# A two-layer decoder trunk on eight cores: small column block first, and the deferred norm steps spread over the next stage

## The reference, cut to what is computed

```
for i in range(2):                                   # layer 0 even mixer, layer 1 odd mixer
    x = x + 0.5 * swiglu(rmsnorm(x, g_ffn[i,0]), ...)        # 1024 -> 2*2816 -> 1024
    h = rmsnorm(x, g_mix[i])
    x = x + (even_mixer(h) if i == 0 else odd_mixer(h))      # pooling + 31-wide conv | 3-wide conv
    x = x + 0.5 * swiglu(rmsnorm(x, g_ffn[i,1]), ...)
    gate = sigmoid(rmsnorm(x, g_ple[i]) @ w_ple_gate[i])
    x = x + gate * rmsnorm(p[i] @ w_ple_proj[i], g_pp[i])
y = rmsnorm(x, g_final)
```

## Time and profile before

| what | value |
|---|---|
| time before, median of 2 runs | 3115.78 us (3113.93 to 3117.63) |
| the profiled execution | 3113.1 us |
| its span on the slowest core (core 3) | 3111.5 us |
| TensorE busy | 2802.3 us, 90% of the span |
| VectorE busy | 1273.6 us, 41% |
| ScalarE busy | 845.9 us, 27% |
| GpSimd busy | 272.7 us, 9% |
| mean granted clock of core 3 | 0.958 |

### The profile page before, as it was taken

How to read it: one execution, slowest core, us unless ns; L and a number is a source line. 1 busy time by engine, 2 the same in 40 slices (tenths; PEclk the granted TensorE clock), 3 DMA queues, 4 the chain that set the end, 5 groups by cost and what they waited for, 6 DMA issues and landing times.

```text
span 3111.5 us, 48681 instructions; the slowest of 8 cores (3096.7 to 3111.5 us)
## 1 busy us (share of the span) xinstructions
PE 2802.3 (90%) x17664; PEld 1507.3 (48%) x17664; DVE 1273.6 (41%) x2357; ACT 845.9 (27%) x1695; POOL 272.7 (9%) x407
## 2 busy tenths in 40 slices
PE   1999997999889999999974999979997999999996
PEld 0455443555345545455432555545554555555553
DVE  4222455232642257523364224542326323762245
ACT  1201334122430122221253113342225202232125
POOL 0000000000220000000031000000003100000003
PEclk9999998999999999999986999989998999999997
DMA  6433401524143534243325443215341533424332
GB/s 139 72 56 64 73 18 28 84 47 71 24 68 52 93 59 71 37 78 59 58 63 124 86 82 57 46 19 88 55 68 25 106 66 68 90 40 86 68 54 66
DMA packets 61386, 202.64 MB, mean 65 GB/s; under 512 B 8160, under 2 KB 14944, under 8 KB 61152
## 3 DMA queue, kind: packets, MB, share of 16 engines
q0 software_dynamic: 44592, 179.16, 34.3%
q1 hardware_dynamic: 16560, 20.36, 2.2%
HBM read 368.97 MB, written 10.62 MB: 122 GB/s over the span
## 4 chain that ended last, share of the span: by engine, by line
PE 81%; DVE 8%; ACT 3%; issue 3%; DMA 2%; SPq 2%; DVEq 0%; ACTq 0%; POOL 0%; POOLq 0%
PE ps L457 81%; DVE h L427 3%; DVE nrs L446 2%; ACT h L420 2%; SPq L464 2%; DMA x<-xT 1%; DVE x L427 1%; ACT scr L420 1%; DVE scr L427 1%; DMA ring<-wts 1%; DVE pts L423 1%; DVE x L423 0%; ACT L420 0%; DVE v L423 0%; DVE lrs L446 0%
## 5 line engine op out<-in xcount | busy, mean ns | idle before, releaser
L457 PE MATMUL ps<-h,ring 128*128 128x512 bf16 (+2 forms) x11352 | 1810.1, 321 | 37.8 <-DVE h L427 17.6
L457 PEld LDWEIGHTS ps<-h,ring 128*128 128x128 bf16 x11352 | 968.1, 99 | 861.9 <-issue 93.1
L420 ACT ACTIVATE scr<-ps 128x512 f32<-128x512 f32 (+2 forms) x858 | 397.7, 473 | 1497.7 <-PE ps L457 1401.7
L423 DVE TENSOR_TENSOR hid<-ps,scr 128x512 bf16<-128x512 f32 (+2 forms) x528 | 282.5, 535 | 984.8 <-PE ps L457 932.4
L457 PE MATMUL ps<-hid,ring 128*128 128x512 bf16 (+2 forms) x4224 | 659.6, 318 | 1.0 <-issue 0.5
L457 PEld LDWEIGHTS ps<-hid,ring 128*128 128x128 bf16 x4224 | 359.1, 99 | 300.4 <-issue 2.3
L464 POOL DMA_DIRECT2D ring<-wts x298 | 157.6, 534 | 2577.4 <-PE ps L457 2550.4
L427 DVE SCALAR_TENSOR_TENSOR x<-ps,x 128x512 f32<-128x512 f32 (+2 forms) x384 | 200.0, 532 | 347.4 <-PE ps L457 345.1
L420 ACT ACTIVATE h<-x 128x512 bf16<-128x512 f32 (+2 forms) x432 | 201.1, 501 | 424.4 <-DVE x L427 268.4
L457 PE MATMUL ps<-h,ones 128*128 128x512 bf16 (+2 forms) x432 | 98.5, 387 | 168.5 <-ACT h L420 168.3
L427 DVE SCALAR_TENSOR_TENSOR h<-x,par,nrs 128x512 bf16<-128x512 f32 (+2 forms) x384 | 214.1, 605 | 8.4 <-DVE nrs L446 4.7
(11 more groups left out here) (63 smaller groups left out, 679.8 us busy)
## 6 DMA issues: line engine op xcount, KB each, us to landing
ring<-wts POOLq DMA_DIRECT2D x216, 512.0 KB, 6.6
ring<-wts POOLq DMA_DIRECT2D x80, 768.0 KB, 7.4
x<-xT SPq DMA_DIRECT2D x32, 256.0 KB, 12.1
yT<-x SPq DMA_DIRECT2D x24, 256.0 KB, 2.0
yT<-x SPq DMA_DIRECT2D x8, 192.0 KB, 2.1
pt<-pT POOLq DMA_DIRECT2D x4, 288.0 KB, 10.8
pt<-pT POOLq DMA_DIRECT2D x4, 256.0 KB, 12.0
yT<-x SPq DMA_DIRECT2D x16, 64.0 KB, 1.6
```

What stands on the lines that cost most here:

```text
L420: S.op("act", lambda e: e.activation(out=out, in_=in_, func=func, **kw), reads=rd, writes=[out])
L423: S.op("dve", lambda e: e.tensor_tensor(out=out, in0=in0, in1=in1, op=op), reads=[in0, in1], writes=[out])
L457: ins = e.matmul(ps_ap, l, r, start=(i == 0), stop=(i == n - 1))
```

## The change

The small block becomes the first of each pass, and in pass 1 the blocks become (0, 128), (128, 384), (512, 512). The flush marker in the order of the input stages goes: a tick follows each item, and a flush stands before the first item of the last block. In `ple` the flush moves from the first chunk of the first block to the start of the last block, ahead of its `PTS` product; all chunks tick. Conditions that named a block by its number name it by its columns.

```
-    G1_BLOCKS = [(0, 512), (512, 384), (896, 128)]
+    G1_BLOCKS = [(0, 128), (128, 384), (512, 512)]
...
     def tb_order(nt, nb):
         lead = min(3, nt)
-        out = [(0, 0), "F"]
+        out = [(0, 0)]
         out += [(0, b) for b in range(1, nb - 1)]
...
             for oi, item in enumerate(order):
-                if item == "F":
+                j, bi = item
+                if bi == nb - 1 or pi > 0:
                     flush()
-                    continue
-                j, bi = item
...
                 dve_tt(HID[:, j, c0:c0 + n], pu[:, 0:n], sg[:, 0:n], ALU.mult)
+                tick()
...
         for bi, blk in enumerate(blocks):
             c0, n = blk
+            if bi == len(blocks) - 1:
+                flush()
             for k in range(2):
                 dve_tt(PTS[:, k, 0:n], PT[:, l * 2 + k, c0:c0 + n], RSE[:, c0:c0 + n], ALU.mult)
...
-                if bi == 0 and mo == 0:
-                    flush()
-                else:
-                    tick()
+                tick()
             x_block_final(blk, next_g)
...
-        blocks = [(0, 512), (512, 512), (1024, 128)] if g == 0 else G1_BLOCKS
+        blocks = [(1024, 128), (0, 512), (512, 512)] if g == 0 else G1_BLOCKS
```

More of the change, by code:

```diff
@@ L608, in last_use @@
         for i, it in enumerate(order):
-            if it != "F":
-                lu[it[0]] = i
+            lu[it[0]] = i
         return lu
@@ L707, in even_mixer @@
         for oi, item in enumerate(order):
-            if item == "F":
+            j, bi = item
+            if bi == nb - 1:
                 flush()
-                continue
-            j, bi = item
             if j not in wts_:
@@ L716, in even_mixer @@
             c0, n = blocks[bi]
-            is_s = (g == 0 and bi == 2)
+            is_s = (g == 0 and c0 == 1024)
             pv, pg = bank(), bank()
@@ L730, in even_mixer @@
                 dve_stt(O_DS[:, j, :], th[:, 0:n], 1.0, vh[:, 0:n], ALU.add, ALU.mult)
-            if last_prompt and bi == nb - 1:
+            if last_prompt and c0 + n == 1024:
                 dve_stt(O_DP[:, j, 0:30], th[:, n - 30:n], 1.0, vh[:, n - 30:n], ALU.add, ALU.mult)
-            if g == 0 and bi == 1:
+            if g == 0 and c0 + n == 1024:
                 dve_stt(UTAIL[:, j, 0:30], th[:, n - 30:n], 1.0, vh[:, n - 30:n], ALU.add, ALU.mult)
+            tick()
             if lu[j] == oi:
@@ L769, in pool_item @@
             dve_stt(H[:, c, c0:c0 + n], src[:, P:L], 1.0 / w, xe[:, P:L], ALU.mult, ALU.subtract)
-            if g == 0 and bi == 0:
+            if g == 0 and c0 == 0:
                 tmp = scratch()
@@ L858, in odd_mixer @@
         for oi, item in enumerate(order):
-            if item == "F":
+            c, bi = item
+            if bi == nb - 1:
                 flush()
-                continue
-            c, bi = item
             if c not in wts_:
```

## The result

The changed kernel took **1.0167** times as long as the kernel before, 95% interval 1.0153 to 1.0181; the execution profiled took 3164.5 us, with a span of 3162.9 us on core 2. The difference is clear of the noise, and under the 2% that the chances were given for. On spans the change is +51.4 us where the sum said +42. So mechanism and sign were as forecast; the largest term was too small by 9.4 us, and three other groups of terms missed by 4 to 10 us each, which happened to cancel.

What follows compares the result with a forecast made beforehand. TensorE, busy 90% of the span, was taken to lose time only at joins between stages. Terms from -6.5 to +27 summed to +42, making the span of 3111.5 us 3153.5; the forecast was 3155 us, range 3122 to 3184.

Steps and rivals of the forecast that it cites:

- The flush ahead of `PTS` is a bare chain: `ple`, layer 0: before the second wide block TensorE waits out a norm chain, 21.2 us; stretch +5.0 pass 0, +4.5 pass 1.
- the deferral: Rival: the flush in `ple` costs nothing and the `ple` and passes terms are given back, -45, 3068 us; chance 0.04.
- the end: End of the kernel: a wide root, reciprocal, 8 scalings and last store follow the last sum, 14.5 us against 8.5; +7.3.
- The change of passes: Pass 0 to pass 1: flushed norm, stores, loads and first norms stand uncovered ahead of the second wide block; +27, bounds +21 to +38.
- The crowded rival: At the passes loads land only when traffic drains, and GpSimd and VectorE slow the chains: +62 or more, 3180 to 3190; chance 0.20.
- FFN to even mixer, -5.0 and -1.8: Join from FFN to even mixer, passes 0 and 1: the small norm sum's wait goes, one wait of about 1 us stays.
- Even mixers, +11: Even mixers, both passes: outputs +6.9 and +6.5 from waits for PSUM banks, pooling and convolution +2.7 and -5.
- the net +2.7: Even mixer, pass 0, pooling and convolution: a new wait of 10.6 us with the clock, against the 6.56 us wait shrinking to 4.
- the 2 us of slow products: Everywhere: about 2 us of products at the lower clock charged behind each TensorE wait of more than 3 us.
- Odd mixers, -6.0 in both: Odd mixers, each pass: outputs -6.5 as the third wait goes, `odd_in` +0.5 (bounds -3 and +8) for norm work not covered.
- The start, -2: Start of the kernel: the second wide block's scalings no longer stand ahead of the first items; -2.
- The rival that waits change places: Mixer terms (+11) come out as nil and loads take their bare 11.1 us: +26, 3125 to 3139 us; chance 0.14.

Runs made afterwards that it cites:

- second profile: The changed kernel unaltered, profiled in a second set of runs: 3161.6 and 3164.0 us, beside 3109 to 3114 us for the kernel before.
- joined version: Changed kernel with only ticks in `ple`, `odd_in` flushing at its first item, pass-1 weights held, `PT` and `UXS` loaded later: 0.9854 of the kernel before, span 3066.1 us.

## Why the prediction was right or wrong, point by point

- **The flush ahead of `PTS` is a bare chain, and the deferral gives nothing back**: right, and shown by taking it out. Chain in layer 0 of pass 0: 21.2 us forecast, 21.6 measured; what it costs there 13.1 and 13.2. The stretches of `ple` in layer 0 (+6.4, +5.5) and the end (+7.0) came within 0.4 us.
- **The change of passes**: mechanism right, one term mis-sized. b's products start 50.2 us after a's end (50 forecast). The step that failed is "the weights now start 15 us before the loads, so I take 16". It looked at the loads and let the stores pass for free: its 36.5 leave 0.5 us between the last scaling and the first load. The loads took 5.2 us, the stores ahead of them 20.6, and from the last scaling to the first square there were 26.5 us where 16.5 were taken. This made b's columns 10.2 us later than said, and the stretch +36.4 (+33.9 in the second profile) in place of +27, near my bound of +38. Holding the weights and `PT` takes 12 to 14 us off it. The crowded rival had this half right (loads at E2 + 44 to 49; b's squares began at E2 + 46.7), and its other half, chains slowed by GpSimd, wrong: they were on time.
- **FFN to even mixer, -5.0 and -1.8**: missed in pass 0. Up to the first product of the convolution (394.77 us before, 394.52 after) the stretch is +1.2, in pass 1 -2.8. The small sum's wait went as said, but a weight tile's 5.64 us took its place. Small items use up weight tiles faster than wide ones (16 products take 1.06 us at 128 columns, 3.62 at 512), and the load of `UXS` stood ahead of that tile on GpSimd's queue. The prediction followed VectorE's queue past every move and not GpSimd's. In the joined version, with `UXS` behind, the same part is -5.7.
- **Even mixers, +11**: missed as well, by as much as the change of passes. From the first product of the convolution on, pass 0 is -0.7 where +9.6 was forecast, and pass 1 +2.1 (+1.5 forecast): +1.5 in all. The waits named came (bank 9.63 and 9.40, pooling 6.96; in pass 1 the pooling cost 3.51 and not 1). In pass 0 the part up to the convolution's end is +5.7 (the pooling term had 10.6), the layer norm's wait -8.5 (7.9 is what the net +2.7 took off, although 6.56 with its splinters and clock shrinking to 4 would give only 6.4), and the outputs +2.1 (+6.9). What did not come is largely the 2 us of slow products charged behind each long wait: TensorE is busy 4.6 us less from 293 to 618 us for the same work, and the granted clock of 470 to 560 is 0.91 and not 0.87 as before. Why it is higher with waits as long stays open.
- **Odd mixers, -6.0 in both**: the sum was -2.0, from -5.5 and +3.5. `odd_in` with its join cost 2.4 and 5.8 us where +0.5 was taken for both (my bound was +8), and the outputs gave 7.9 and 2.3 where 6.5 was taken for both. The estimate for `odd_in` was the same for both passes; in pass 1 the items before b's are 384 wide and cover less VectorE work, so the scratch wait is 6.16 us and not 3.89. With the flush behind the first item in the joined version the two stretches win 5.8 and 6.9 more.
- **The start, -2**: -1.5.
- **The sum**: the misses of the small terms (+0.5, -4.0, +0.4, -2.5, -0.4, 0, +6.5, -0.3 by stretches) add up to next to nothing, so that the total's miss of 9.4 is that of the passes. By terms they are larger: the joins +5.2, the even mixers -9.5, the odd mixers +4.0. That they cancel is luck; a sum that fits is not a proof of its terms.
- **The rival that waits change places** lost as a whole, for the passes; but its first half, that the even mixers' +11 come out as nil, was nearer (+1.5) than my term. Changing the even mixer's order moved 16 us of waits to other rows and won nothing, as it says.

Open: the two profiles of the changed kernel differ by 2.5 us at the passes, which I did not resolve; and the four waits for weights in the small blocks of `ple` (15.7 us together in the changed kernel) were left as they are, one of 4.16 us still standing in the joined version in `ple` of layer 1, pass 0.

## What to carry to other kernels

A flush of deferred work ahead of an operation on which the next products depend turns deferred work into a bare chain. Spread it by ticks under a wide block that is left, as here, and put no flush between the two widest blocks. When a step is moved, follow each queue that it is moved past, DMA queues too, and each transfer on the chain, the store ahead of a load as well as the load. Two edits can cost more together than apart (-27 and +25 gave +51), so cost a change of order together with the flushes that stand in it.

## What the runs showed of the hardware that I had not expected

Eight stores of 256 KB on SP's queue land in 2.3 to 3.6 us (medians) with nothing of GpSimd's queue beside them, in 13.7 beside six weight tiles of 512 KB, and in 20.6 beside these and `PT`; eight stores of only 64 KB took 20.0 beside the same traffic (one profile). The eight loads behind the stores took 5.2 and 4.5 us where they were issued as the weights ran out, 6.5 with the weights held, and 12.9 in the kernel before, where they and not the stores stood beside the weights. Of two transfers that depend on each other, the slow one here was each time the one that met the traffic, not the later one.
